# The inverse sums of the decay heads go through DRAM, and the last values step moves into the next head

## The chip, the cores and the metric

The kernel runs on one core of a Trainium2 chip. The metric is the device time of one launch in microseconds, the median of three runs. A core has five engines that run their own instruction streams and meet at semaphores: TensorE (PE; the weight loads are listed as PEld), VectorE (DVE), ScalarE (ACT), GpSimd (POOL) and SyncE (SP), which issues all transfers of this kernel.

## The reference, cut to what matters

The program is a transformer block followed by a two-layer second block over 1024 tokens of width 1024. The change lies in the second layer of the second block, in its attention with forget gates: 16 heads of width 64, causal, with a decay term per key that comes from a running sum of log forget gates.

```python
def forgetting_attention(u, k, v, cum):
    # logit[t,s] = q_t.k_s/sqrt(Dh) + cum[t] - cum[s], causal, swept in 128-query blocks
    ...
        logits = jnp.einsum('bqhd,bkhd->bhqk', qi, k,
                            preferred_element_type=jnp.float32) * scale
        logits = logits + (ci[..., :, None] - cum_k[:, :, None, :])
        ...
        p = jax.nn.softmax(logits, axis=-1)
        return jnp.einsum('bhqk,bkhd->bqhd', p.astype(v.dtype), v)

def mixer_sublayer(x, mem, w_in, w_mem_kv, w_out, main_fn):
    ...
    y_main = main_fn(u_main)
    y_mem = memory_attention(q_mem, mem, w_mem_kv)
    y = jnp.concatenate([y_main * jax.nn.silu(g_main), y_mem * jax.nn.silu(g_mem)], axis=-1)
    return y @ w_out
```

## The kernel before, in words

Everything but the row maxima and row sums is held with features on the partitions. Products are made of float32 numbers split into a high and a low part (`whi`, `wlo` for weights, `Hb[0]`, `Hb[1]` for activations), so that one product is three matmuls (`mm3`, lines 428 to 430). GpSimd splits each weight panel of 128x1024 (`split`, lines 844 and 846) after SP has loaded it (`load_panel`, line 462).

The stage `fox` runs the 16 heads one after the other, about 31.5 us each. A head has 8 query tiles `qt` of 128 queries. For each tile TensorE makes the scores (`scores`, lines 1680 and 1681, with the mask at 1683), VectorE takes the row maximum against the decay row `ncB` (`row_max`, line 3026), ScalarE makes exponentials with their row sums (`exps`, through the helper on line 1815), TensorE turns them back by transposes (`flips`, line 1694), ScalarE copies the high part (`flip_hi`), VectorE makes the low part (`flip_lo`, line 2324), and for each pair of tiles TensorE multiplies by the values (`values(h, p)`, p from 0 to 3, line 1708). The result of a pair lies in two halves of one PSUM bank; ScalarE copies one (`other_half`), VectorE adds both into `Y32` (`add`, line 2327). Two heads share one 128-partition block of `Y32`.

Between these steps TensorE is filled with steps of later projections: `fill(n)` takes n steps of three matmuls each from the tiles that make the next keys, queries and gates. How many stand where is written in the table `FILL` (24 per head, 4 of them behind the first scores), and `FILL_LAST` (16) for the last two heads. Evacuating these tiles is `project` on ScalarE and VectorE; its last step for a key half is the cast on line 2998.

At the end of a head VectorE takes the reciprocals of the 8 row sums of each partition (line 3078, `inv_sum`, which lies in `stat_pool`). Queries are on partitions there but along the free dimension in `Y32`. So TensorE makes 8 transposes of broadcast columns (`inverse_rows`, line 1717) into two banks of PSUM, then `values(h, 3)` follow, and VectorE multiplies the 64x1024 block of the head by the turned rows (line 2327, second use). After two heads `gate(i)` (line 3048) multiplies the 128x1024 block by its gate; it stands behind query tile 1 of the next even head.

SP's queue in a head holds the values of the next head (`Vx`, line 793), a weight panel, and the decay row of the next head (`ncB`, line 798), which may go only when the head's last row maximum is taken. Transfers wait on SP in the order in which they are written.

## Time and profile before

| | us |
|---|---|
| median of 3 runs | 3052.43 (3050.56 to 3052.73) |
| the profiled execution | 3051.6 |
| its span | 3049.8 |

| engine | busy us | share of the span |
|---|---|---|
| PE | 2938.5 | 96% |
| PEld | 2444.0 | 80% |
| DVE | 1519.9 | 50% |
| POOL | 1032.7 | 34% |
| ACT | 923.2 | 30% |

Times on rows are counted from the start of the span. The decay heads run from about 2270 to 2765 us. Matmuls are pipelined: each row of one gives its start and its own length, which overlaps the next one's; what a matmul costs in a row of others is the distance between two starts. "idle before <-releaser" in brackets on a row is a wait and the engine and line that ended it.

### The profile page before, as it was taken

How to read it: one execution, taken by the hardware profiler on the slowest of the kernel's cores; microseconds unless marked ns; L12 is line 12 of the kernel's file. 1: busy time of each engine (PE TensorE's matmuls, PEld its weight loads, DVE VectorE, ACT ScalarE, POOL GpSimd, SP SyncE). 2: the span in 40 equal slices, each digit the busy share in tenths (PEclk: the TensorE clock that was granted, in tenths of full speed). 3: DMA queues.
4: the chain of work that ended last, by engine and by line, in shares of the span. 5: the costliest groups of instructions: out<-in, count | busy, mean ns of one | idle time of the engine just before them, and what ended most of it. 6: DMA issues, size and time to landing. Idle time of an engine off the chain costs nothing.

```text
span 3049.8 us, 37301 instructions
## 1 busy us (share of the span) xinstructions
PE 2938.5 (96%) x14926; PEld 2444.0 (80%) x14926; DVE 1519.9 (50%) x2288; ACT 923.2 (30%) x1606; POOL 1032.7 (34%) x454
## 2 busy tenths in 40 slices
PE   7999999999999999999999999999999999999997
PEld 3877778888887888888888887788788888887786
DVE  5943238887634313132234444545536666664545
ACT  5122226665113101010010111411335555553412
POOL 1333251000586434444444443233331221212241
PEclk9999999999999999999999999999999999999998
DMA  6534584221533111111111111111232212111111
GB/s 243 190 121 140 202 239 117 73 73 42 191 120 111 49 49 48 50 47 51 46 50 47 55 63 49 42 49 42 98 125 63 56 56 63 56 56 43 36 53 63
DMA packets 118090, 256.85 MB, mean 84 GB/s; under 512 B 47228, under 2 KB 69276, under 8 KB 113712
## 3 DMA queue, kind: packets, MB, share of 16 engines
q1 hardware_dynamic: 117936, 254.71, 25.5%
q8 instruction: 107, 1.75, 0.2%
q14 instruction: 47, 0.39, 0.0%
HBM read 210.20 MB, written 45.97 MB: 84 GB/s over the span
## 4 chain that ended last, share of the span: by engine, by line
PE 81%; DVE 8%; ACT 5%; issue 2%; DMA 1%; POOL 1%; SPq 0%; ACTq 0%; DVEq 0%; POOLq 0%
PE ps L428 23%; PE ps L430 23%; PE ps L429 23%; PE ps L1708 2%; ACT tmp L1815 2%; PE ps L1285 2%; PE ps L1694 2%; PE ps L1273 1%; ACT Ea L1815 1%; PE ps L1680 1%; PE ps L1681 1%; DVE tmp L2549 1%; DVE Z L2327 1%; DVE mx L2778 1%; DVE ETb_lo L2324 1%
## 5 line engine op out<-in xcount | busy, mean ns | idle before, releaser
L844 POOL TENSOR_TENSOR whi<-raw,onesf 128x1024 fp32r<-128x1024 f32 x189 | 365.0, 1931 | 1888.7 <-PE ps L430 1766.5
L428 PE MATMUL ps<-Hb_hi,whi 128*128 128x512 f32 x1424 | 573.3, 403 | 10.3 <-DVE Y L2751 5.9
L430 PE MATMUL ps<-Hb_hi,wlo 128*128 128x512 f32 x1424 | 556.4, 391 | 0.0
L429 PE MATMUL ps<-Hb_lo,whi 128*128 128x512 f32 x1424 | 555.5, 390 | 0.0
L846 POOL TENSOR_TENSOR wlo<-raw,whi 128x1024 fp32r<-128x1024 f32 x189 | 504.2, 2668 | 14.8
L428 PEld LDWEIGHTS ps<-Hb_hi,whi 128*128 128x128 f32 x1424 | 268.3, 188 | 62.6 <-issue 8.1
L430 PEld LDWEIGHTS ps<-Hb_hi,wlo 128*128 128x128 f32 x1424 | 267.6, 188 | 57.9
L429 PEld LDWEIGHTS ps<-Hb_lo,whi 128*128 128x128 f32 x1424 | 268.6, 189 | 47.8
L1815 ACT ACTIVATE tmp<-ps 64x256 f32<-64x256 f32 (+2 forms) x97 | 57.8, 596 | 531.9 <-PE ps L430 465.0
L1815 ACT ACTIVATE tmp<-tmp,mx 128x1280 f32<-128x1280 f32 (+2 forms) x192 | 187.2, 975 | 66.9 <-DVE mx L3026 56.8
L428 PE MATMUL ps<-Uhi,whi 128*128 128x512 f32 x512 | 199.2, 389 | 0.0
L429 PE MATMUL ps<-Ulo,whi 128*128 128x512 f32 x512 | 199.2, 389 | 0.0
L430 PE MATMUL ps<-Uhi,wlo 128*128 128x512 f32 x512 | 199.2, 389 | 0.0
L2327 DVE TENSOR_TENSOR tmp<-tmp 128x1024 f32<-128x1024 f32 x44 | 86.1, 1957 | 184.0 <-ACT tmp L1815 183.6
L2698 DVE SCALAR_TENSOR_TENSOR X<-ps,modx,X 128x1024 f32<-128x1024 f32 x32 | 41.1, 1283 | 256.6 <-PE ps L430 256.6
L428 PE MATMUL ps<-Yb_hi,whi 128*128 128x512 f32 (+1 forms) x408 | 153.8, 377 | 0.0
L429 PE MATMUL ps<-Yb_lo,whi 128*128 128x512 f32 (+1 forms) x408 | 153.6, 377 | 0.0
L430 PE MATMUL ps<-Yb_hi,wlo 128*128 128x512 f32 (+1 forms) x408 | 153.6, 377 | 0.0
L428 PE MATMUL ps<-Hhi,whi 128*128 128x512 f32 x384 | 151.9, 395 | 1.0 <-POOL wlo L846 0.8
L429 PE MATMUL ps<-Hlo,whi 128*128 128x512 f32 x384 | 149.6, 390 | 0.0
L430 PE MATMUL ps<-Hhi,wlo 128*128 128x512 f32 x384 | 149.5, 389 | 0.0
L1815 ACT ACTIVATE Ea<-ps 128x512 fp32r<-128x512 f32 (+1 forms) x192 | 87.2, 527 | 83.3 <-PE ps L1273 83.3
(458 smaller groups left out, 5816.9 us busy)
## 6 DMA issues: line engine op xcount, KB each, us to landing
raw<-in_w SPq DMA_DIRECT2D x197, 512.0 KB, 3.5
adas<-in_ada SPq DMA_DIRECT2D x16, 1024.0 KB, 4.9
raw<-in_w SPq DMA_DIRECT2D x44, 256.0 KB, 3.8
adaE<-in_ada SPq DMA_DIRECT2D x4, 2048.0 KB, 23.4
gate_d<-gst SPq DMA_DIRECT2D x16, 512.0 KB, 2.8
v_d<-VS SPq DMA_DIRECT2D x2, 4096.0 KB, 14.9
ncB<-cum_d SPq DMA_DIRECT2D x16, 512.0 KB, 3.5
Vx<-v_d SPq DMA_DIRECT2D x16, 512.0 KB, 4.5
```

The costliest lines, as they stand in the source:

```text
L428: nc.tensor.matmul(o, wh, xh, start=start, stop=False)
L429: nc.tensor.matmul(o, wh, xl, start=False, stop=False)
L430: return nc.tensor.matmul(o, wl, xh, start=False, stop=stop)
L844: nc.gpsimd.tensor_tensor(whi[b][:, 0:w], raw[b][:, 0:w], onesf[:, 0:1].to_broadcast([P, w]), ALU.mult).then_inc(S("split_hi"), 1)
L846: nc.gpsimd.tensor_tensor(wlo[b][:, 0:w], raw[b][:, 0:w], f32(whi[b][:, 0:w]), ALU.subtract).then_inc(S("split"), 1)
L1273: last = nc.tensor.transpose(ps[:, c:c + P], tmp[t % 2][:, P * kt:P * kt + P], ident[:, :])
L1285: last = nc.tensor.matmul(o, Va[h % 2][:, kt, :], Ea[u % 2][n][:, kt, :], start=kt == 0 and n == 0, stop=kt == 9 and n == 1)
L1694: last = nc.tensor.transpose(ps[:, b + P * (kt - 4 * x):b + P * (kt - 4 * x) + P], tmp[qt % 2][:, P * kt:P * kt + P], ident[:, :])
L1708: last = nc.tensor.matmul(ps[:, 5 * HALF + c0:5 * HALF + CTX], Vx[h % 2][:, kt, :], E[x][:, kt, c0:CTX], start=kt == 0 and x == 0, stop=kt ...
L1815: nc.scalar.activation(dst, src, func, **kw).then_inc(sem, 1)
L2327: nc.vector.tensor_tensor(o, a, b, op).then_inc(sem, 1)
L2698: nc.vector.scalar_tensor_tensor(X1[:, k, :], g, modx[:, 40 + k:41 + k], X1[:, k, :], ALU.mult, ALU.add).then_inc(free, 1)
```

## The change

Heads 0 to 14 no longer turn their inverse sums on TensorE. SP stores the 128x8 reciprocals of a head into a row of DRAM (`inv_d`) in the order of the queries, and loads them back broadcast over 64 partitions, 256 queries at a time, into spare columns of `rs` and `acc` (`rowB`), two pieces for each half of the queries. GpSimd multiplies `Y32` by them in four pieces of 64x256 (`normalise`), placed between its weight splits (`heads_beside`). The second half's loads wait until GpSimd has used the first half's.

`values(h, 3)` now stands in head h + 1, behind its first scores and two of the four projection steps there; `other_half(h, 3)` and `add(h, 3)` move with it on ScalarE and VectorE. `gate(i)` moves from query tile 1 to the end of query tile 7 of the same head and waits for GpSimd's multiplies. Head 15 keeps its transposes and its multiply on VectorE.

```diff
+                def store_inverse(h):
+                    sp.wait_ge(S("fx_inv"), h + 1)
+                    sp.dma_start(inv_d[h].rearrange("(t p) -> p t", p=P), inv_sum[:, 8 * (h % 2):8 * (h % 2) + 8], allow_slow_non_contiguous=True).then_inc(S("row_stored"), 16)
+
+                def inverse_rows(h, half):
+                    r = slice(64 * (h % 2), 64 * (h % 2) + 64)
+                    if half == 0:
+                        sp.wait_ge(S("row_stored"), 32 + 16 * (h + 1))
+                    if h or half:
+                        sp.wait_ge(S("fx_norm"), 4 * h + 2 * half)
+                    for x in range(2):
+                        c = HALF * half + CTX * x
+                        sp.dma_start(rowB[x][r, :], inv_d[h:h + 1, c:c + CTX].to_broadcast([64, CTX])).then_inc(S("inv_row"), 16)
...
                 for h in range(FOX):
+                    if h:
+                        store_inverse(h - 1)
                     if h + 1 < FOX:
                         head_values(h + 1)
+                    if h:
+                        inverse_rows(h - 1, 0)
                     if h % 2 == 0:
+                        if h:
+                            inverse_rows(h - 1, 1)
                         load_panel("fox", 25, 0, kq_panel(h + 1))
                     elif h + 1 < FOX:
                         load_panel("fox", 25, 0, gate_panel(h // 2 + 1))
+                        inverse_rows(h - 1, 1)
+                    else:
+                        inverse_rows(h - 1, 1)
                     if h + 1 < FOX:
                         head_decay(h + 1)
...
+            def normalise(h, half, last_split):
+                r = slice(64 * (h % 2), 64 * (h % 2) + 64)
+                gp.wait_ge(S("inv_row"), 32 * (2 * h + half + 1))
+                gp.wait_ge(S("fx_out"), 3 * (4 * h + 2 * half + 2))
+                gp.wait_ge(S("split"), last_split + 1)
+                for x in range(2):
+                    c = slice(HALF * half + CTX * x, HALF * half + CTX * x + CTX)
+                    y = Y32[r, h // 2, c]
+                    nc.gpsimd.tensor_tensor(y, y, rowB[x][r, :], ALU.mult).then_inc(S("fx_norm"), 1)
+                    gp.wait_ge(S("fx_norm"), 4 * h + 2 * half + x + 1)
+
+            def heads_beside(p0):
+                for m in range(2, 4):
+                    split(p0 + m)
+                for i in range(8):
+                    if i:
+                        normalise(2 * i - 1, 0, p0 + 3 * i + 3)
+                        normalise(2 * i - 1, 1, p0 + 3 * i + 3)
+                    split(p0 + 3 * i + 4)
+                    if i < 7:
+                        split(p0 + 3 * i + 5)
+                    normalise(2 * i, 0, p0 + (3 * i + 5 if i < 7 else 25))
+                    normalise(2 * i, 1, p0 + (3 * i + 5 if i < 7 else 25))
+                    split(p0 + (3 * i + 6 if i < 7 else 26))
...
-                        if h and c == 1:
-                            pe.wait_ge(S("fx_inv"), 3 * h)
...
-                        if qt < 7:
+                        if qt == 0 and h:
+                            fill(2)
+                            values(h - 1, 3)
+                            fill(share[0] - 2)
+                        elif qt < 7:
                             fill(share[qt])
...
-                    inverse_rows(h)
-                    if h == FOX - 1:
-                        next(ahead)
-                    values(h, 3)
+                inverse_rows(FOX - 1)
+                next(ahead)
+                values(FOX - 1, 3)
...
                 def gate(i):
-                    dve.wait_ge(S("fx_inv"), 3 * (2 * i + 2))
+                    dve.wait_ge(S("fx_norm"), 4 * min(2 * i + 2, FOX - 1))
...
                         if qt == 0:
                             for x in before:
                                 project(*x)
+                            if h:
+                                add(h - 1, 3)
...
-                        if qt == 1 and h % 2 == 0 and h:
+                        if qt == 7 and h % 2 == 0 and h:
                             gate(h // 2 - 1)
                     x = slice(8 * (h % 2), 8 * (h % 2) + 8)
                     dve.wait_ge(S("fx_e"), 8 * h + 8)
+                    if h >= 2:
+                        dve.wait_ge(S("row_stored"), 32 + 16 * (h - 1))
                     nc.vector.reciprocal(inv_sum[:, x], row_sum[:, x]).then_inc(S("fx_inv"), 1)
                     for x in range(2):
                         flip_lo(h, 7, x)
-                    add(h, 3)
-                    dve.wait_ge(S("fx_inv"), 3 * h + 2)
-                    dve.wait_ge(S("fx_out"), 3 * (4 * h + 4))
-                    tt(Y32[r, h // 2, :], Y32[r, h // 2, :], ps[r, HALF:HALF + T], ALU.mult, S("fx_inv"))
```

TensorE's order at the end of head 1 and the start of head 2, before (L1694 flips, L1717 the transposes of the inverse sums, L1708 values, L1680 to L1683 scores, L428 to L430 one projection step):

```order
L1694 MATMUL ps<-ident,tmp 128x128 x8
L428 MATMUL ps<-Hb_hi,whi 128x512
L429 MATMUL ps<-Hb_lo,whi 128x512
L430 MATMUL ps<-Hb_hi,wlo 128x512
L1717 MATMUL ps<-ident,stat_pool 128x128 x8
L1708 MATMUL ps<-ETb_hi,Vx_189 128x256
L1708 MATMUL ps<-ETb_lo,Vx_189 128x256
...
L1680 MATMUL ps<-K_0_184,Q_0_182 128x128
L1681 MATMUL ps<-K_0_186,Q_0_182 128x128
L1683 MATMUL ps<-mrow_60,identr 128x128
L428 MATMUL ps<-Hb_hi,whi 128x512
```

The same place after (L1744 flips, L1758 values, L1730 to L1733 scores, L430 to L432 one projection step):

```order
L1744 MATMUL ps<-ident,tmp 128x128 x8
L430 MATMUL ps<-Hb_hi,whi 128x512
L431 MATMUL ps<-Hb_lo,whi 128x512
L432 MATMUL ps<-Hb_hi,wlo 128x512
L1730 MATMUL ps<-K_0_184,Q_0_182 128x128
L1731 MATMUL ps<-K_0_186,Q_0_182 128x128
L1733 MATMUL ps<-mrow_60,identr 128x128
L430 MATMUL ps<-Hb_hi,whi 128x512
...
L1758 MATMUL ps<-ETb_hi,Vx_189 128x256
L1758 MATMUL ps<-ETb_lo,Vx_189 128x256
```

The transposes are gone, and between the last projection step of head 1 and the sixteen value matmuls stand the first scores of head 2 and two projection steps.

VectorE's order at the end of head 2 and the start of head 3, before (L2998 the cast, L3078 the reciprocal, L2324 the low parts, L2327 the addition and then the multiply, L3026 the row maximum of head 3):

```order
L2998 CAST K_1_187<-K_1_187 64x512
L3078 RECIPROCAL stat_pool<-mxf 128x8
L2324 TENSOR_TENSOR ETb_lo<-ps,ETb_hi 128x4x128 x2
L2327 TENSOR_TENSOR Y_167<-ps,tmp 64x256
L2327 TENSOR_TENSOR Y_167<-Y_167,ps 64x1024
L3026 ISA tmp,mx<-ps,ncB 128x128
L3026 ISA mx 128x1
L3012 SCALAR_TENSOR_TENSOR acc<-acc,ps 128x512
```

The same place after (L3053 the cast, L3105 the gate, L3138 the reciprocal, L2379 the low parts, L3081 the row maximum, L2382 the addition):

```order
L3053 CAST K_1_187<-K_1_187 64x512
L3105 SCALAR_TENSOR_TENSOR Y_167<-Y_167,acc 128x1024
L3138 RECIPROCAL stat_pool<-mxf 128x8
L2379 TENSOR_TENSOR ETb_lo<-ps,ETb_hi 128x4x128 x2
L3081 ISA tmp,mx<-ps,ncB 128x128
L3081 ISA mx 128x1
L3067 SCALAR_TENSOR_TENSOR acc<-acc,ps 128x512
L2382 TENSOR_TENSOR Y_167<-ps,tmp 64x256
```

The gate has come in ahead of the reciprocal, the multiply is gone, and the addition stands behind head 3's first row maximum and a projection's evacuation.

SP's order in head 2, after (L804 the store of head 1's reciprocals, L795 the values of head 3, L814 the broadcast loads, L464 a weight panel, L800 the decay row of head 3):

```order
L804 DMA inv_d<-stat_pool 128x8x1
L795 DMA Vx_189<-v_d 128x1024
L814 DMA rs<-inv_d 64x256
L814 DMA acc<-inv_d 64x256
L814 DMA rs<-inv_d 64x256
L814 DMA acc<-inv_d 64x256
L464 DMA raw<-in_w 128x1024
L800 DMA ncB<-cum_d 128x1024
```

Before, the values, the panel and the decay row stood there alone.

## Rows read from the trace of the kernel before

**Rows 1.** The page, part 1: busy us of each engine (share) xinstructions.

```profile
PE 2938.5 (96%) x14926; PEld 2444.0 (80%) x14926; DVE 1519.9 (50%) x2288; ACT 923.2 (30%) x1606; POOL 1032.7 (34%) x454
```

**Rows 2.** Stretch: length, busy PE, PEld, DVE, ACT, POOL (instructions), clock, DMA.

```profile
2334.00:2366.00 32.00, 31.93 (x193) 27.88 (x192) 20.63 (x51) 17.75 (x39) 4.85 (x3) 1.00 0.17 56
```

**Rows 3.** Line 1717: count, duration ns min/median/max, first and last start us.

```profile
L1717 PE MATMUL ps<-ident,stat_pool x128: 271/273/323, 2292.8 to 2765.7; 128*128 128x128 f32 x128
```

**Rows 4.** Timeline of TensorE, seam of heads 1 and 2: start us, us, instruction.

```profile
2324.22 1.04 PE L1717 MATMUL ps<-ident,stat_pool 128*128 128x128 f32 x8
2325.33 0.38 PE L1708 MATMUL ps<-ETb_hi,Vx 128*128 128x256 f32 x1
...
2327.28 0.27 PE L1680 MATMUL ps<-K,Q 128*128 128x128 f32 x1
...
2327.61 0.45 PE L428 MATMUL ps<-Hb_hi,whi 128*128 128x512 f32 x1
...
2329.05 0.39 PE L428 MATMUL ps<-Hb_hi,whi 128*128 128x512 f32 x1
```

**Rows 5.** The chain that ended last, same seam: start us, us, what.

```profile
2323.35 0.61 ACT ETb_hi L1815
2323.98 1.30 DVE ETb_lo L2324 x2
```

**Rows 6.** Timeline of SP and VectorE, seam of heads 1 and 2.

```profile
2321.10 0.33 SPq L798 DMA_DIRECT2D ncB<-cum_d  x1
...
2323.24 0.42 DVE L2998 CAST K<-K 64x512 fp32r<-64x512 f32 x1
...
2329.22 1.26 SPq L462 DMA_DIRECT2D raw<-in_w  x2
```

**Rows 7.** Timeline of GpSimd, VectorE and TensorE, seam of heads 2 and 3.

```profile
2342.67 1.90 POOL L844 TENSOR_TENSOR whi<-raw,onesf 128x1024 fp32r<-128x1024 f32 x1 [13.47 <-PE ps L430]
...
2354.80 0.42 DVE L2998 CAST K<-K 64x512 fp32r<-64x512 f32 x1
...
2355.25 0.20 DVE L3078 RECIPROCAL stat_pool<-mxf 128x8 f32<-128x8 f32 x1
...
2355.55 1.29 DVE L2324 TENSOR_TENSOR ETb_lo<-ps,ETb_hi 128x512 fp32r<-128x512 f32 x2
...
2355.79 1.04 PE L1717 MATMUL ps<-ident,stat_pool 128*128 128x128 f32 x8
2356.89 0.38 PE L1708 MATMUL ps<-ETb_hi,Vx 128*128 128x256 f32 x1
```

**Rows 8.** Timeline of VectorE: the gate multiply of the first pair.

```profile
2333.46 1.22 DVE L3048 SCALAR_TENSOR_TENSOR Y<-Y,rs 128x1024 f32<-128x1024 f32 x1
```

**Rows 9.** Timeline of VectorE and TensorE, seam of heads 14 and 15.

```profile
2733.04 0.42 DVE L2998 CAST K<-K 64x512 fp32r<-64x512 f32 x1
...
2733.75 1.09 PE L1717 MATMUL ps<-ident,stat_pool 128*128 128x128 f32 x8 [0.45 <-DVE stat_pool L3078]
...
2736.88 0.27 PE L1680 MATMUL ps<-K,Q 128*128 128x128 f32 x1
```

**Rows 10.** GpSimd's groups by shape: count, busy us, mean ns, idle before.

```profile
L844 POOL TENSOR_TENSOR whi<-raw,onesf 128x1024 fp32r<-128x1024 f32 x189 | 365.0, 1931 | 1888.7 <-PE ps L430 1766.5 <-DMA raw<-in_w 96.0 <-DVE Hb_lo L2324 26.2
...
L862 POOL TENSOR_TENSOR rsr<-raw,onesf 128x1024 fp32r<-128x1024 f32 x1 | 2.9, 2877 | 0.0
L864 POOL TENSOR_TENSOR tmpr<-raw,rsr 128x512 fp32r<-128x512 f32 x2 | 2.6, 1294 | 0.2
L864 POOL TENSOR_TENSOR QN_lo<-raw,rsr 128x1024 fp32r<-128x1024 f32 x1 | 2.4, 2392 | 0.1
```

**Rows 11.** DMA issues: count, KB each, median us from issue to landing.

```profile
raw<-in_w SPq DMA_DIRECT2D x44, 256.0 KB, 3.8
...
ncB<-cum_d SPq DMA_DIRECT2D x16, 512.0 KB, 3.5
...
v_d<-vst SPq DMA_DIRECT2D x5, 1024.0 KB, 6.7
```

More of the change, by code:

```diff
@@ L340, in build @@
         SG = (rs, acc)
+        rowB = (rs[:, T:KEYS], acc[:, T:KEYS])
         neg_max, row_sum, inv_sum = mx, mxf, stat_pool
@@ L364, in build @@
         cum_d = scratch("cum_d", FOX, T)
+        inv_d = scratch("inv_d", FOX, T)
         wb_d, w64_d, wf_d = scratch("wb_d", P, 8, 2 * P), scratch("w64_d", 96, T), scratch("wf_d", 8, P, 4, P)
@@ L642, in sp_program @@
                         sp.wait_ge(S("rates"), 9)
-                        sp.dma_start(rate_d.rearrange("h (t p) -> (h t) p", p=P), krows[0:NH * 10, :]).then_inc(S("rate_stored"), 16)
+                        sp.dma_start(rate_d.rearrange("h (t p) -> (h t) p", p=P), krows[0:NH * 10, :]).then_inc(S("row_stored"), 16)
             if on("mla"):
@@ L666, in sp_program @@
                 sp.wait_ge(S("kr_stored"), 32)
-                sp.wait_ge(S("rate_stored"), 16)
+                sp.wait_ge(S("row_stored"), 16)
                 sp.wait_ge(S("wf_moved"), STAGED)
@@ L780, in sp_program @@
                 load_panel("foxw", 4, 0, 0)
-                sp.wait_ge(S("cum"), 1)
-                sp.dma_start(cum_d, ncum[0:FOX, :]).then_inc(S("cum_stored"), 16)
+                sp.wait_ge(S("gate_log"), 4)
+                sp.dma_start(cum_d, ncum[0:FOX, :]).then_inc(S("row_stored"), 16)
                 for j in range(1, 4):
@@ L786, in sp_program @@
                 sp.dma_start(v2_d[1], f32(VS[1][:, :, :, :])).then_inc(S("fx_vst"), 16)
-                sp.wait_ge(S("cum_stored"), 16)
+                sp.wait_ge(S("row_stored"), 32)
             if on("fox"):
@@ L922, in pool_program @@
                         splits(stage, 0, 12 - SPLIT_LEAD)
+                    elif stage == "fox":
+                        heads_beside(P0["fox"])
                     elif stage == "out1":
@@ L1439, in mem_tiles @@
                             elif l:
-                                pe.wait_ge(S("fx_inv"), 3 * FOX)
+                                pe.wait_ge(S("fx_inv"), FOX + 2)
                             c = slice(HALF * x, HALF * x + HALF)
@@ L1712, in inverse_rows @@
                 def inverse_rows(h):
-                    pe.wait_ge(S("fx_inv"), 3 * h + 1)
+                    pe.wait_ge(S("fx_inv"), h + 1)
                     pe.wait_ge(S("fx_x"), CHUNKS * h + CHUNKS)
@@ L2268, in project @@
                     else:
-                        act.wait_ge(S("cum"), 1)
+                        act.wait_ge(S("gate_log"), 4)
                         if x >= 2:
@@ L2310, in act_program @@
                                 project(*x)
+                            if h:
+                                other_half(h - 1, 3)
                         if qt in (2, 5) and mine:
@@ L2313, in act_program @@
                     flip_hi(h, 7)
-                    other_half(h, 3)
+                other_half(FOX - 1, 3)
             if on("mem2"):
@@ L2981, in dve_program @@
                 dve.wait_ge(S("gate_log"), 3)
-                nc.vector.tensor_tensor_scan(ncum[r, :], rs[r, 0:T], acc[r, 0:T], 0.0, ALU.mult, ALU.add).then_inc(S("cum"), 1)
+                nc.vector.tensor_tensor_scan(ncum[r, :], rs[r, 0:T], acc[r, 0:T], 0.0, ALU.mult, ALU.add).then_inc(S("gate_log"), 1)
                 token_values(1)
@@ L3045, in gate @@
                 def gate(i):
-                    dve.wait_ge(S("fx_inv"), 3 * (2 * i + 2))
+                    dve.wait_ge(S("fx_norm"), 4 * min(2 * i + 2, FOX - 1))
+                    if i == 7:
+                        dve.wait_ge(S("fx_inv"), FOX + 2)
                     dve.wait_ge(S("fx_g"), 2 * i + 2)
@@ L3052, in dve_program @@
                 for h in range(FOX):
-                    r = slice(64 * (h % 2), 64 * (h % 2) + 64)
                     before = projections(h - 1)[2:] if h else []
@@ L3065, in dve_program @@
                                 project(*x)
+                            if h:
+                                add(h - 1, 3)
                         if qt == 2 and mine:
@@ L3080, in dve_program @@
                         flip_lo(h, 7, x)
-                    add(h, 3)
-                    dve.wait_ge(S("fx_inv"), 3 * h + 2)
-                    dve.wait_ge(S("fx_out"), 3 * (4 * h + 4))
-                    tt(Y32[r, h // 2, :], Y32[r, h // 2, :], ps[r, HALF:HALF + T], ALU.mult, S("fx_inv"))
+                add(FOX - 1, 3)
+                dve.wait_ge(S("fx_inv"), FOX + 1)
+                dve.wait_ge(S("fx_out"), 12 * FOX)
+                tt(Y32[64:128, 7, :], Y32[64:128, 7, :], ps[64:128, HALF:HALF + T], ALU.mult, S("fx_inv"))
                 gate(7)
```

## The prediction

> **What bounds the kernel now.** I read the page's busy shares first: TensorE is busy 96% of the 3049.8 us, VectorE 50%, ScalarE 30%, GpSimd 34% [rows 1]. The change touches only the stage with the sixteen decay heads, so the next view is that of a stretch: between 2334 and 2366 us (one head and a bit) TensorE is busy 31.93 of 32.00 us at full granted clock, while VectorE works 20.6 us, ScalarE 17.8 us and GpSimd 4.9 us [rows 2]. A microsecond taken from TensorE's row is worth a microsecond here, as long as nothing else becomes late; a microsecond taken from VectorE or given to GpSimd is worth nothing by itself.
>
> Third, the seam between two heads, in order of time. Each head ends with eight transposes of the inverse sums (L1717, sixteen times eight of them, 273 ns each [rows 3]). Matmuls are pipelined, so their price is not 8 x 273 ns = 2.18 us but the distance between starts: the transposes at 2324.22, the first value matmul at 2325.33 [rows 4]. That is 1.11 us from the transposes' start to the values' start. And the transposes are not even what the values wait for: the chain that ended last goes through ScalarE's copy of the last flips (2323.35) and VectorE's two subtractions (2323.98, 1.30 us), and then to the values [rows 5]. The reader is to see in this that deleting the transposes alone would gain nothing at such a seam, since the values would still start at about 2325.3. It is the second part of the change, values moved behind the next head's first scores, that makes the 1.11 us free.
>
> **What is removed and moved on TensorE.** Fifteen of sixteen heads lose the eight transposes; the last head keeps them. At fifteen seams the values step now stands behind the next head's first scores and two projection steps. These three are no new work: the scores took 2327.61 - 2327.28 = 0.33 us, the two steps 2329.05 - 2327.61 = 1.44 us [rows 4]. So TensorE, at 2324.22, does the scores and two steps and comes to the values at 2324.22 + 0.33 + 1.44 = 2325.99, when the subtractions, over at 2323.98 + 1.30 = 2325.28, have long released them [rows 5]. It asks for them 0.7 us after they are free. The whole 1.11 us is gained (1.10 at the seam between heads 2 and 3 [rows 7]), provided that the next head's scores may start 3.06 us earlier than before. They need the last cast of the keys: 2323.24 + 0.42 = 2323.66, 0.56 us before TensorE wants it [rows 6]. The first row maximum then needs the decay row, whose transfer is issued at 2321.10 [rows 6] and lands 3.5 us later [rows 11], at 2324.6, before VectorE is free (2325.3). The exponentials it feeds are wanted by the next flips only some 4 us on. So no new wait at a seam of this kind.
>
> **The gate multiply, moved.** On VectorE the gate (128x1024, 1.22 us [rows 8]) leaves the second query tile of heads 2, 4 ... 14 for the end of the eighth, ahead of the reciprocal and of the last subtractions. There it is in the way. At the seam behind head 2 the cast ends at 2355.22; with the gate behind it (2356.44), the reciprocal (0.20, 2356.64) and the subtractions (1.29) end at 2357.93 instead of 2356.84 [rows 7]. TensorE comes to the values at 2355.79 + 0.33 + 1.44 = 2357.56. It waits about 0.4 us, so that 1.10 - 0.4 = 0.7 us is left. That holds for heads 2 to 12, six seams.
>
> Head 14 has fewer projection steps, and TensorE waits there already: the transposes stood back 0.45 us for the reciprocal, the values step ended at 2736.88 [rows 9], and scores and two steps would have been done at 2736.88 + 0.33 + 1.44 = 2738.65. Now: cast until 2733.46, gate until 2734.68, reciprocal 2734.88, subtractions 2736.15, values (1.95 us, from 2325.33 to 2327.28 in [rows 4]) until 2738.15. The gain is 0.5 us.
>
> **The multiply by the inverse sums** leaves VectorE (64x1024 per head) and needs no cover: VectorE is busy two thirds of the time here [rows 2]. On GpSimd it becomes four multiplies of 64x256 per head, a shape that the trace does not have. A two-input op takes 1294 ns for 512 elements and 2392 ns for 1024 [rows 10], that is 2.14 ns per element and, carried down, 0.75 us for 256; bounds are 0.6 us (half of 1294) and 1.3 us. Four are 3.0 us a head. GpSimd waited 13.5 us for TensorE before the split at 2342.67 [rows 7], so the splits keep room. No TensorE time.
>
> **The way through DRAM.** SP now issues per head one store of 128x8 values, four bytes each, and four loads of 64 rows. Behind the waiting SP stand the next weight panel and the next head's decay row. The even heads are the tight ones: the store of head h-1 stands behind the panel loads, issued at 2329.22 for 1.26 us [rows 6], so it starts at 2330.5. Nearest row for 1024 short pieces: a quarter-megabyte panel in 256-byte pieces lands in 3.8 us; a store of one megabyte takes 6.7 us [rows 11]. I take 3.8 and keep 3 and 6.7. Then 2334.3; the first two rows land by 2337.8 (at most the decay row's 3.5 us), two multiplies until 2339.3, the other two rows 2342.8, two multiplies 2344.3. The gate asks for them at 2355.2 [rows 7]. There are 10.9 us to spare, so nothing is lost for any store under 3.8 + 10.9 = 14.7 us. The odd heads' chain ends ahead of the decay row's issue, which is a whole head later. Cost on the path: nothing.
>
> **The sum.** Eight seams without a gate (behind heads 0, 1, 3, 5 ... 13) x 1.10 = 8.8; six x 0.7 = 4.2; one x 0.5. Together 13.5 us. The profiled execution took 3051.6 us (span 3049.8), hence 3038.1; the median of the three runs is 0.8 above it, so the median should be 3038.5 to 3039. I say **3038.5**, 0.45% faster.
>
> **A rule that speaks against it.** The trace has a split of 128x1024 on GpSimd that took 2877 ns where the same op takes about 1930 in the mean [rows 10], so GpSimd does get held up by about 0.95 us elsewhere in the program. The Trainium skill, SBUF — State Buffer, section SBUF: two separate sides, says that GpSimd and VectorE share a port pair as an exclusive lock, taken for a whole instruction, which VectorE wants in a 2-port mode or with two SBUF inputs; its gate multiply is such an instruction. By that rule the gate would be blocked if a multiply of GpSimd ran at that moment. No row of the decay heads shows a collision.
>
> **Rivals.** (a) *The seam fills up again.* The values leave the wait, but the cover is thin: 0.56 us between cast and scores, 0.7 us between subtractions and values. If the subtractions come 1.0 us later against TensorE than I count (ScalarE does the next exponentials sooner, VectorE the next maxima), each seam loses 0.3 us without a gate and 1.0 with one: 8 x 0.3 + 7 x 1.0 = 9.4, leaving 4 us, time 3048; half of that gives 3043. For it: TensorE follows VectorE closely at each seam [rows 5]. Against it: VectorE sheds 1.22 + 1.2 us in each pair's early part. (b) *The DRAM chain comes too late,* the slower side. If four-byte stores cost over 14.7 us, VectorE stands at the gate with the last subtractions and the next maximum behind it, and TensorE behind those, in seven heads. At 20 us: 7 x 5.3 = 37 us lost, 13.5 gained, 3076. At 16.6 us it breaks even. For it: no row has four-byte pieces. Against: 1024 pieces of 256 bytes need 3.8 us. (c) *Collisions on VectorE:* if a multiply of GpSimd holds the gate for 0.75 us in seven heads, 7 x 0.75 = 5.3 us go, time 3044. Against: by the chain above GpSimd is done ten microseconds earlier. (d) *The gate costs nothing,* if the subtractions wait for ScalarE in any case: 15 x 1.1 = 16.5, time 3035.5.
>
> **How the numbers follow.** Forecast 0.62; (a) 0.15, of which a third ends within 0.2%; (b) 0.08; (c) 0.05; (d) 0.10. The range takes in the forecast, (d), (c) and the milder half of (a): 3034.5 to 3046. What a measurement can tell from no change is 0.2%, 6.1 us, so faster means below 3046.3. Faster 0.85, same 0.07, slower 0.08.
>
> **What would show it.** L1717's successor with 8 transposes instead of 128. From the last projection matmul of a head to the next head's first scores 0.2 us. A wait of TensorE for VectorE's subtractions of about 0.4 us in even heads and none in odd ones. The store landing in 3 to 7 us, and GpSimd's multiplies at 0.75 us, over by the middle of the head. VectorE idle at the gate for DMA or GpSimd would prove (b); cast and gate longer than 0.42 and 1.22 us would prove (c); waits for the subtractions at every seam, (a). The forecast is wrong at its root if a head still takes 31.5 us, the distance from 2324.22 to 2355.79 [rows 4, 7].

## The result, and the profile after

| | us |
|---|---|
| before, median of 5 runs | 3050.66 (3047.43 to 3052.73) |
| after, median of 5 runs | 3063.78 (3062.64 to 3067.46) |
| ratio | 1.0046 (95%: 1.0035 to 1.0058) |
| the profiled execution of after; its span | 3066.08; 3064.3 |

The change costs 13 us; the prediction's sum was a gain of 13.5 us. The page of after, part 1 and the line on packets in part 2, beside [rows 1]:

```profile
PE 2930.4 (96%) x14806; PEld 2437.3 (80%) x14806; DVE 1519.1 (50%) x2273; ACT 922.6 (30%) x1606; POOL 1078.3 (35%) x514
...
DMA packets 138490, 260.84 MB, mean 85 GB/s; under 512 B 63788, under 2 KB 89676, under 8 KB 134112
```

TensorE has 120 instructions and 8 us of work less, in a span 14.5 us longer. So it idles more, and the question is where. The best ruler is the distance between the ends of two heads, each end taken as the start of the last row of eight flips on TensorE's timeline (L1694 before, L1744 after): head 3 stands for the distance from head 2's end to head 3's. Fifteen distances in each trace, in us:

| | head 1 | head 2 | head 3 | head 5 | head 7 | heads 9, 11 | sum of 15 |
|---|---|---|---|---|---|---|---|
| before | 31.45 | 31.56 | 31.46 | 31.45 | 31.45 | 31.4 | 471.5 |
| after | 30.27 | 30.58 | 40.70 | 38.79 | 40.66 | 31.3 | 487.2 |

Odd seams (behind heads 1, 3 ...) gained 1.0 to 1.6 us each (2.6 behind head 13), about what was promised or more. The loss sits at the even seams, between an even head and the next odd one, above all at the first three. The waits of after between 2270 and 2790 us (engine, line, releaser: us in total, times, longest):

```profile
POOL Y L885 <- DMA acc<-inv_d: 180.0, 27, 15.6
...
DVE tmp L3081 <- DMA ncB<-cum_d: 34.3, 7, 8.7
...
PE ps L1744 <- ACT tmp L1868: 19.6, 7, 5.7
...
PE ps L1758 <- DVE ETb_lo L2379: 10.2, 7, 2.2
```

VectorE stands seven times, 34 us in all, before the first row maximum of an odd head, because the decay row is not there. Behind the first three of these waits TensorE stands for the exponentials, 15.9 us in all (and 0.4 us behind head 14; the other three waits of that line, 3.3 us at heads 14 and 15, stand in the kernel before too). In all seven places it waits for the subtractions. GpSimd's own 180 us are the cause of nothing by their size; it is their place that matters. The chain that ended last in after, from the odd seam to the even one (start us, us, what):

```profile
2323.11 1.91 POOL whi L869
2325.08 2.42 POOL wlo L871
2327.51 0.58 SPq L464
2328.14 0.67 SPq L464
2328.85 9.80 DMA inv_d<-stat_pool
2338.67 0.48 SPq L814
2339.20 3.12 DMA acc<-inv_d
2342.38 0.75 POOL Y L885
2343.21 0.75 POOL Y L885
2343.97 0.45 SPq L814
2344.46 3.29 DMA acc<-inv_d
2347.87 0.73 POOL Y L885
2348.69 0.74 POOL Y L885
2349.50 1.91 POOL whi L869
2351.47 2.39 POOL wlo L871
2353.88 0.34 SPq L464
2354.27 11.11 DMA ncB<-cum_d
2365.40 0.29 DVE tmp L3081
```

This is the working of the prediction's DRAM part, row for row, with two differences. The store takes 9.80 us and not 3.8. And the chain does not end at the gate: GpSimd's split of the next panel (L869, L871) stands in GpSimd's order behind the four multiplies, SP's next panel load (L464) waits for that split to free the raw buffer, and the decay row stands in SP's queue behind the panel. So the decay row is issued at 2354.27, 2.5 us after the head's last flips began (2351.78); at the odd seam before it went at 2319.62, 1.6 us ahead of them (2321.20). And it then takes 11.11 us to land instead of 3.5 [rows 11].

VectorE and TensorE at that seam (timeline of after; idle time and releaser in brackets):

```profile
2351.47 2.38 POOL L871 TENSOR_TENSOR wlo<-raw,whi 128x1024 fp32r<-128x1024 f32 x1
2351.93 0.42 DVE L2382 TENSOR_TENSOR Y<-ps,tmp 64x256 f32<-64x256 f32 x1 [0.65 <-ACT tmp L1868]
2352.38 1.76 DVE L3053 CAST K<-K 64x512 fp32r<-64x512 f32 x1
...
2356.72 0.39 PE L1758 MATMUL ps<-ETb_hi,Vx 128*128 128x256 f32 x1 [1.50 <-DVE ETb_lo L2379]
...
2365.40 0.29 DVE L3081 CUSTOM_DVE_ANT_0 tmp<-ps,ncB 128x128 f32<-128x128 f32 x1 [8.74 <-DMA ncB<-cum_d]
...
2366.29 0.47 PE L1744 MATMUL ps<-ident,tmp 128*128 128x128 f32 x1 [5.72 <-ACT tmp L1868]
```

The cast took 0.42 us before [rows 7] and 1.76 now: it ends at 2354.14, 0.28 us after GpSimd's split (2353.86). Then TensorE's clock (stretches of after; columns as in rows 2):

```profile
2358.00:2366.00 8.00, 2.57 (x17) 2.16 (x15) 0.30 (x2) 0.26 (x1) 0.00 (x0) 0.97 0.58 46
2366.00:2370.00 4.00, 3.71 (x10) 2.94 (x11) 1.56 (x5) 1.98 (x7) 0.00 (x0) 0.50 0.34 86
2370.00:2374.00 4.00, 4.00 (x17) 3.35 (x16) 0.99 (x3) 1.10 (x4) 1.90 (x1) 0.71 0.00 0
2374.00:2378.00 4.00, 4.00 (x21) 3.38 (x20) 1.94 (x4) 1.75 (x4) 3.75 (x3) 1.00 0.02 4
```

After the 5.72 us of idleness the granted clock is 0.50 (1.2 GHz) and it is back at 1.00 (2.4 GHz) after 2372: two projection matmuls stood 0.43 us apart until then, 0.23 after it. Six microseconds at half speed cost 3.

The 40.70 us of head 3 are so accounted for: a wait for the subtractions of 1.50 us where the kernel without the way through DRAM (the first experiment below) has 0.16, so 1.3 more, as much as the cast is longer (1.76 - 0.42); 5.7 of idleness; 3.0 of half clock; together 10.0. An undisturbed head of this kind takes 30.7 there, and 40.7 - 30.7 = 10.0.

### The profile page after: what moved, and what is told of

Its sections match the earlier page's. It is cut to its first block, busy times and chain, and to the rows that moved or that the text cites. A ratio compares the mean times of both kernels' runs of the same rounds, so it can differ in the third digit from the quotient of the medians.

```text
span 3064.3 us, 37209 instructions
## 1 busy us (share of the span) xinstructions
PE 2930.4 (96%) x14806; PEld 2437.3 (80%) x14806; DVE 1519.1 (50%) x2273; ACT 922.6 (30%) x1606; POOL 1078.3 (35%) x514
## 2 busy tenths in 40 slices
DMA packets 138490, 260.84 MB, mean 85 GB/s; under 512 B 63788, under 2 KB 89676, under 8 KB 134112
## 4 chain that ended last, share of the span: by engine, by line
PE 75%; DVE 9%; DMA 5%; ACT 5%; issue 3%; POOL 2%; SPq 1%; ACTq 0%; DVEq 0%; POOLq 0%
PE ps L430 22%; PE ps L432 21%; PE ps L431 21%; ACT tmp L1868 2%; PE ps L1337 2%; PE ps L1744 1%; PE ps L1325 1%; PE ps L1758 1%; DMA inv_d<-stat_pool 1%; DMA ncB<-cum_d 1%; ACT Ea L1868 1%; DVE tmp L2604 1%; DMA acc<-inv_d 1%; POOL wlo L871 1%; PE ps L1730 1%
## 5 line engine op out<-in xcount | busy, mean ns | idle before, releaser
L869 POOL TENSOR_TENSOR whi<-raw,onesf 128x1024 fp32r<-128x1024 f32 x189 | 366.2, 1937 | 1676.7 <-PE ps L432 1552.5
L430 PE MATMUL ps<-Hb_hi,whi 128*128 128x512 f32 x1424 | 576.5, 405 | 10.3 <-DVE Y L2806 5.9
L432 PE MATMUL ps<-Hb_hi,wlo 128*128 128x512 f32 x1424 | 558.6, 392 | 0.0
L871 POOL TENSOR_TENSOR wlo<-raw,whi 128x1024 fp32r<-128x1024 f32 x189 | 504.0, 2667 | 14.8
L430 PEld LDWEIGHTS ps<-Hb_hi,whi 128*128 128x128 f32 x1424 | 270.0, 190 | 62.4 <-issue 8.1
L432 PEld LDWEIGHTS ps<-Hb_hi,wlo 128*128 128x128 f32 x1424 | 268.8, 189 | 58.5
L430 PE MATMUL ps<-Uhi,whi 128*128 128x512 f32 x512 | 199.2, 389 | 0.0
L432 PE MATMUL ps<-Uhi,wlo 128*128 128x512 f32 x512 | 199.2, 389 | 0.0
L2382 DVE TENSOR_TENSOR tmp<-tmp 128x1024 f32<-128x1024 f32 x44 | 86.1, 1957 | 184.1 <-ACT tmp L1868 183.6
L430 PE MATMUL ps<-Yb_hi,whi 128*128 128x512 f32 (+1 forms) x408 | 153.8, 377 | 0.0
L432 PE MATMUL ps<-Yb_hi,wlo 128*128 128x512 f32 (+1 forms) x408 | 153.6, 377 | 0.0
L430 PE MATMUL ps<-Hhi,whi 128*128 128x512 f32 x384 | 152.1, 396 | 0.5 <-POOL wlo L871 0.2
L432 PE MATMUL ps<-Hhi,wlo 128*128 128x512 f32 x384 | 149.5, 389 | 0.0
L3081 DVE CUSTOM_DVE_ANT_0 tmp<-ps,ncB 128x512 f32<-128x512 f32 (+3 forms) x128 | 75.0, 586 | 98.0 <-PE ps L1733 51.8
```

Source lines behind the costliest of these rows:

```text
L430: nc.tensor.matmul(o, wh, xh, start=start, stop=False)
L432: return nc.tensor.matmul(o, wl, xh, start=False, stop=stop)
L869: nc.gpsimd.tensor_tensor(whi[b][:, 0:w], raw[b][:, 0:w], onesf[:, 0:1].to_broadcast([P, w]), ALU.mult).then_inc(S("split_hi"), 1)
L871: nc.gpsimd.tensor_tensor(wlo[b][:, 0:w], raw[b][:, 0:w], f32(whi[b][:, 0:w]), ALU.subtract).then_inc(S("split"), 1)
L2382: nc.vector.tensor_tensor(o, a, b, op).then_inc(sem, 1)
L3081: nc.vector.tensor_tensor_reduce(tmp[qt % 2][:, c0:c1], ps[:, b:b + c1 - c0], ncB[:, c0:c1], -1.0, col_ if x else 3e38, ALU.add, ALU.min, ...
```

## The experiments

Three theories. **A, the order:** the decay row is late since it stands behind a panel load that waits for a split that waits for the multiplies. **B, the store:** 1024 pieces of four bytes take too long, and slow the transfers beside them. **C, the collision:** the split that comes late now runs beside VectorE's last cast (and gate), which then stand until it ends. All ratios are against the kernel before on the same chip. Times on rows of different kernels have no common zero inside the decay heads (head 1's last flips begin at 2322.66 before and at 2321.20 in after), so where two kernels are compared, places are given from the start of a head's last flips.

**The seam alone.** The changed kernel without store, loads and GpSimd's multiplies:

```diff
-                        store_inverse(h - 1)
...
-                        inverse_rows(h - 1, 0)
...
-                            inverse_rows(h - 1, 1)
...
-                        normalise(2 * i - 1, 0, p0 + 3 * i + 3)
...
-                    dve.wait_ge(S("fx_norm"), 4 * min(2 * i + 2, FOX - 1))
+                    dve.wait_ge(S("fx_out"), 3 * (4 * (2 * i + 1) + 4))
```

> The changed kernel without the way of the inverse sums: no store, no broadcast loads, no multiply on GpSimd (so heads 0 to 14 are left undivided), the gate waits for nothing but the additions. The order on TensorE and VectorE is that of the change. If the prediction's step on the seams holds and all the loss is in the chain through DRAM, this gains the 13.5 us that I forecast, ratio to before 0.9956, TensorE waits about 0.4 us for the subtractions in even heads, and the cast takes 0.42 us. If the new seam itself costs time (maxima and exponentials late), it stays above 0.998 with waits at most seams.

3035.23 us, 0.9947 (0.9930 to 0.9963), 16.7 us faster. Heads take 30.25 to 30.27 us where no gate stands at the seam (30.57 once, behind head 1) and 30.64 to 30.69 where one does (the last two, with fewer projection steps, apart), 454.1 in sum against 471.5. Heads 0 to 14 stay undivided here. The half of the change that lies on TensorE is worth all that was forecast and more; all that went wrong is in the way through DRAM.

**The transposes alone.** The kernel before with one transpose in place of eight in heads 0 to 14; VectorE multiplies these heads by 1.0 instead of the turned rows, so they stay undivided:

```diff
-                    for qt in range(8):
+                    for qt in (range(8) if h == FOX - 1 else range(1)):
```

> The kernel before, with one transpose of the inverse sums instead of eight in heads 0 to 14 and nothing moved. VectorE multiplies these heads by 1.0 instead of the turned rows (so they stay undivided), a shorter operation that nothing waits for. It tests the step that deleting the transposes alone gains nothing: the values step still waits for the subtractions, heads' ends stay 31.5 us apart, time 3050. If the transposes were on the path by themselves, seven of them less at 0.11 us each give 15 x 0.8 = 12 us, time 3038.

3051.27 us against 3051.52, 0.9998 (0.9988 to 1.0007), heads 472.0 in sum. The reading of [rows 5] holds: TensorE merely waits where it transposed (L1708 for L2324, 12.5 us in 15 waits).

**Order on SP (A without C).** In even heads the decay row goes ahead of the panel:

```diff
-                        load_panel("fox", 25, 0, kq_panel(h + 1))
...
                         head_decay(h + 1)
-                        if h % 2:
-                            load_panel("fox", 25, 0, kq_panel(h + 1))
+                        load_panel("fox", 25, 0, kq_panel(h + 1))
```

> The changed kernel, with one move on SP: in even heads the next decay row is issued ahead of the weight panel. Theory A (SP's queue: the decay row stands behind a panel load that waits for GpSimd's late split): the row is issued at the head's last maximum, 4 us sooner, lands in about 3.5 us, VectorE waits for it nowhere; the 16 us of TensorE waiting for exponentials and some 8 us at the low clock go, time about 3041. Theory B (the transfer itself is stretched to 10 us or more by the four-byte store issued behind it): the landing stays near 10 us, VectorE still waits 3 to 5 us in three heads, time above 3052. Under both the cast stays stretched to 1.8 us and TensorE waits 1.5 us for the subtractions in even heads.

3058.58 us, 1.0027 (1.0017 to 1.0036). The decay row is issued at 2351.48 and nobody waits for it any more, yet only 5 of the 28 us between the change and the seam alone came back (8 of the 33 us by the distances: 478.9 in sum). Its timeline at two even seams:

```profile
2353.15 2.38 POOL L869 TENSOR_TENSOR wlo<-raw,whi 128x1024 fp32r<-128x1024 f32 x1
...
2353.61 2.20 DVE L3051 CAST K<-K 64x512 fp32r<-64x512 f32 x1
...
2355.85 1.22 DVE L3103 SCALAR_TENSOR_TENSOR Y<-Y,rs 128x1024 f32<-128x1024 f32 x1
...
2358.40 0.39 PE L1756 MATMUL ps<-ETb_hi,Vx 128*128 128x256 f32 x1 [1.94 <-DVE ETb_lo L2377]
...
2613.23 0.52 DVE L3051 CAST K<-K 64x512 fp32r<-64x512 f32 x1
...
2613.54 2.46 POOL L869 TENSOR_TENSOR wlo<-raw,whi 128x1024 fp32r<-128x1024 f32 x1
2613.78 3.31 DVE L3103 SCALAR_TENSOR_TENSOR Y<-Y,rs 128x1024 f32<-128x1024 f32 x1
...
2618.41 0.38 PE L1756 MATMUL ps<-ETb_hi,Vx 128*128 128x256 f32 x1 [2.30 <-DVE ETb_lo L2377]
```

Either the cast stands (2.20 us instead of 0.42, over 0.28 us after the split's end at 2355.53), or, where the split begins a little later, the cast goes in between the two ops of the split and the gate stands (3.31 instead of 1.22, over 1.09 after 2616.00). The first happens behind heads 2 and 12, the second behind the other five. Each time the subtractions behind them are late by about the same amount, and TensorE waits 17.5 us in seven places. Six of these waits are followed by 3.4 us at half clock, with less idleness than in after (1.9 to 3.2 us each). The stretch behind the first of them, columns as in rows 2:

```profile
2358.00:2366.00 8.00, 7.60 (x36) 6.69 (x37) 2.33 (x8) 2.24 (x7) 0.00 (x0) 0.79 0.49 53
```

A head costs 34.0 to 35.1 us in five of the seven places (32.2 and 33.2 in the others) where 30.7 would do. So A's own wait is a part of the loss, but taking it away lets C's grow, from 10.2 to 17.5 us of waits for the subtractions, and some 23 of the 28 us stay.

By the Trainium skill (SBUF — State Buffer, section SBUF: two separate sides) GpSimd and VectorE hold a shared port pair for whole instructions, which VectorE needs in its 2-port modes and with two SBUF inputs. The trace agrees: cast and gate stand, while the addition at 2351.93 above, whose one input is in PSUM, took its usual 0.42 us beside the split.

**A store of 128 pieces (B).** The reciprocals are stored in the order in which they lie, 32 bytes per partition; this kernel's inverse rows are in the wrong order of queries.

```diff
-                    sp.dma_start(inv_d[h].rearrange("(t p) -> p t", p=P), inv_sum[...
+                    sp.dma_start(inv_d[h].rearrange("(p t) -> p t", p=P), inv_sum[...
```

> The changed kernel with the store laid out by partition: 128 pieces of 32 bytes instead of 1024 of 4 bytes. The rows that come back are in another order, so the output is not the reference's. If the four-byte pieces are what costs 9.8 us, the store lands in 2 to 3 us, the chain ends 7 us sooner, the split starts by 2344 and the decay row goes at the last maximum; no wait for it, no cast beside a split, time 3037 to 3040. If instead the write to DRAM and the wait for it cost most of the 9.8 us whatever the pieces, the landing stays above 7 us and the time near 3060.

3036.20 us, 0.9952 (0.9935 to 0.9969). DMA issues of it and of after, 2260 to 2790 us (count, KB each, median us to landing):

```profile
Vx<-v_d SPq DMA_DIRECT2D x15, 512.0 KB, 3.8
...
inv_d<-stat_pool SPq DMA_DIRECT2D x15, 4.0 KB, 1.9
```

```profile
inv_d<-stat_pool SPq DMA_DIRECT2D x15, 4.0 KB, 9.8
Vx<-v_d SPq DMA_DIRECT2D x15, 512.0 KB, 9.7
```

The same 4 KB land in 1.9 us instead of 9.8, the values beside them in 3.8 instead of 9.7, and the whole loss is gone: the multiplies end at 2341.55 and the split begins at 2341.62. That is 20.7 us behind the start of head 1's last flips, where after has 28.3, the kernel before 20.0 and the kernel with the seam alone, without any multiplies, 18.7.

**The store away from the decay row (B).** The store goes behind the values of the next head, so that it does not run beside the decay row:

```diff
-                    if h:
-                        store_inverse(h - 1)
                     if h + 1 < FOX:
                         head_values(h + 1)
+                    if h:
+                        store_inverse(h - 1)
```

> The changed kernel with the store of the inverse sums behind the load of the next values on SP, instead of ahead of it; the panel and the decay row keep their places. Behind an even head the store then goes about 3 us later, when the decay row has had 4.6 us. Theory B (the store beside it stretches the decay row): the row lands in about 5 us instead of 10 to 11, VectorE's waits of 7.5 to 8.7 us fall to about 3. Theory A (only the late issue counts): landing stays at 10 to 11 us, no change. The chain starts 1 us later in odd heads, so the issue of the decay row is no earlier. Time: 3055 under B, 3064 under A.

3068.98 us, 1.0052 (1.0036 to 1.0069): a miss for the time. The decay row behind head 2, issued at 2356.31, was used at 2360.96, 4.65 us later; the landings of the seven rows are 4.2 to 6.1 us, where the first three of after have 9.9 to 11.1. So the store beside it does stretch its landing. But the store itself now takes 11.1 us in the median beside the values, the panel behind the split leaves 4.5 us behind the start of head 2's last flips instead of 2.1 in after, and what was gained in the wait for the decay row (26.5 us in seven, from 34.3) went into the wait for the subtractions (18.9 us, from 10.2).

**Order on GpSimd (A at its root).** The four-byte store stays; the split goes between the two halves of the multiply, alone and together with the decay row first:

```diff
                         normalise(2 * i - 1, 0, p0 + 3 * i + 3)
-                        normalise(2 * i - 1, 1, p0 + 3 * i + 3)
                     split(p0 + 3 * i + 4)
+                    if i:
+                        normalise(2 * i - 1, 1, p0 + 3 * i + 4)
```

> The changed kernel with the one move on GpSimd alone: the split of the even heads between the two halves of the multiply. SP's order is the change's. If the root is the split that stands behind the whole multiply, this alone brings the panel load, the decay row (issued at the last maximum, near 2350) and the cast back into place: the decay row then has the panel 3 us ahead of it and the four-byte store 5 us behind it and lands in under 5 us; time 3036 to 3039. If SP's order is a cause of its own, waits of VectorE for the decay row of 2 us or more stay and the time is above 3043.

> The changed kernel with two moves: the decay row ahead of the panel load on SP in even heads, and on GpSimd the even heads' split between the two halves of the multiply instead of behind both. The four-byte store stays and lands in about 10 us. Theory C (what is left of the loss once the decay row is on time is the split that now runs beside VectorE's cast and the clock that falls after TensorE's wait): the split is over by 2350, the cast takes 0.42 us before the seam, TensorE waits under 0.5 us for the subtractions, clock as before, time 3036 like the kernel without the chain. Theory D (the slow store itself holds TensorE or VectorE up): still 3050 or more.

Alone 3035.30 us, 0.9951 (0.9935 to 0.9968); with both 3034.27, 0.9943 (0.9927 to 0.9960). GpSimd, SP and VectorE of the first at the even seam (timeline):

```profile
2344.98 2.38 POOL L871 TENSOR_TENSOR wlo<-raw,whi 128x1024 fp32r<-128x1024 f32 x1
...
2347.39 0.34 SPq L464 DMA_DIRECT2D raw<-in_w  x1
...
2347.78 0.43 SPq L800 DMA_DIRECT2D ncB<-cum_d  x1
...
2349.56 0.42 DVE L3054 CAST K<-K 64x512 fp32r<-64x512 f32 x1
```

Two lines moved, and the store may be as slow as it likes (10.8 us here): the split is over 2.2 us before the cast, which takes 0.42 us again, and the decay row leaves SP 1.8 us ahead of the cast, where after has it 1.9 us behind. VectorE still waits for the decay row twice in the first kernel (3.3 us together), TensorE never because of it. The intervals of the two overlap; the second move adds nothing that can be told.

**The slow store in the kernel before.** Only the store and its waits are added:

```diff
+                    if h:
+                        sp.wait_ge(S("fx_inv"), 3 * (h - 1) + 1)
+                        sp.dma_start(inv_d[h - 1].rearrange("(t p) -> p t", p=P), ...
```

> The kernel before, with nothing but the store of the inverse sums added, 1024 pieces of four bytes per head, at the place of SP's queue where the change has it; nobody reads it. It prices the store by itself. Expected: it lands in 9 to 11 us, with nothing of the chain around it; the values' load issued behind it takes 9 to 10 us instead of 4.5, which nobody waits for; decay rows, issued ahead of it, land in 3.5 us; time as before, 3051. If the store holds up the decay row also when nothing else is late, the row's landing goes above 6 us and VectorE waits for it.

3051.60 us, 0.9997 (0.9987 to 1.0006). The store lands in 10.9 us and makes the values land in 10.5 instead of 4.4, and nobody waits. A slow transfer by itself costs nothing here; what hangs on it does.

**A good short store.** As with the 128 pieces above, but GpSimd reads its operands with the matching stride, so that all of the computation is there (each piece then covers part of every query tile, so the multiplies wait for all four additions of the head); and the same with the gate behind the last subtractions:

```diff
+                    p_ = 64 * half + 32 * x
+                    y = Y32[r, h // 2, :].rearrange("f (t p) -> f t p", p=P)[:, :, p_:p_ + 32]
+                    row = rowB[x][r, :].rearrange("f (p t) -> f t p", t=8)
...
-                        if qt == 7 and h % 2 == 0 and h:
-                            gate(h // 2 - 1)
...
                         flip_lo(h, 7, x)
+                    if h % 2 == 0 and h:
+                        gate(h // 2 - 1)
```

> The changed kernel with a store of 128 pieces of 32 bytes, and GpSimd picking the queries back into order in its multiply: 64 rows of 8 x 32 elements, the inverse sums read with a stride of 8. Each piece covers 32 queries of every tile, so the first half waits for all four additions. The output is the reference's. Expected: store 1.9 us as in the run with the long store, multiply 0.75 us, or up to 1.5 if GpSimd is slower with strides, which nothing waits for; time 3036, ratio 0.995. If the strided multiply takes over 3 us each, the split moves late again and the time is above 3045.

> The kernel of the run before, with the gate of the even heads behind the last subtractions instead of ahead of the reciprocal. It prices the gate at its place: the distance of heads' ends was 30.67 us for even heads against 30.26 for odd ones without the chain. If the gate is the 0.4 us, the two become equal and seven seams give 2.8 us, time 3033.5. If the next head's first maximum, now 1.2 us later, is waited for, the even heads stay at 30.67 or grow.

3034.10 us, 0.9945 (0.9928 to 0.9961), the multiplies 0.90 to 0.91 us instead of 0.73; and **3030.22 us**, 0.9933 (0.9916 to 0.9949), the lowest median of all, 20 us under the kernel before; its interval overlaps with those of the next two kernels. With the gate last the even seams fall from 30.65 to 30.27 us, so the gate ahead of the subtractions cost 0.4 us each.

**Late split and slow store, but room behind them (C).** Decay row first and gate last, the split as late as in after; and the same with the last cast on ScalarE (only this move is shown; the other two are as above):

```diff
+                        if qt == 7 and mine and mine[1][0] == "kq":
...
+                            act.wait_ge(S("fx_kqd"), 4 * kx + 2 * ks + 1)
+                            copy(K2[kx % 2][64:128, kc], f32(K2[kx % 2][0:64, kc]), S("fx_kd2"))
...
-                    else:
+                    elif part == 2:
```

> The same without the move of the cast: decay row first, gate behind the subtractions, cast on VectorE. It separates the two. The cast still ends only when GpSimd's operation ends, so I expect it at 1 to 2.2 us in even heads; the subtractions follow 1.1 us sooner than with the gate ahead of them, TensorE waits 0.5 to 2 us, time 3038 to 3045. If the cast is held up by something else than GpSimd (the gate behind it, a queue), it falls to 0.42 us.

> The run with the decay row first (3058.6), where the split of the even heads still runs late, at the end of the eighth tile, with both VectorE operations that got stuck beside it taken away from the place ahead of the subtractions: the last cast of a head is done by ScalarE, and the gate stands behind the subtractions. The split and the four-byte store stay as they were. If what holds the seam is VectorE's copy held up by GpSimd's split, TensorE's waits for the subtractions (1.6 to 3.2 us, seven times) and the low clock behind them go, time 3032 to 3036. If the late split or the slow store hurts in another way, 3045 or more stays.

3033.04 us, 0.9936 (0.9919 to 0.9952), and 3032.05, 0.9934 (0.9917 to 0.9950). The second confirms C: no VectorE instruction that the split can hold stands before the subtractions, and all even seams of heads 2 to 12 take 30.3 us. The store is as slow as before: its trace has no landing times of it, but the first broadcast load, which waits for it, goes 10.1 to 13.6 us behind its issue. The first came out better than I had expected (3038 to 3045). Its timeline:

```profile
2352.89 1.89 POOL L867 TENSOR_TENSOR whi<-raw,onesf 128x1024 fp32r<-128x1024 f32 x1
...
2354.49 0.57 DVE L3051 CAST K<-K 64x512 fp32r<-64x512 f32 x1
...
2354.86 2.47 POOL L869 TENSOR_TENSOR wlo<-raw,whi 128x1024 fp32r<-128x1024 f32 x1
...
2355.22 1.29 DVE L2377 TENSOR_TENSOR ETb_lo<-ps,ETb_hi 128x512 fp32r<-128x512 f32 x2
2356.43 1.98 DVE L3103 SCALAR_TENSOR_TENSOR Y<-Y,rs 128x1024 f32<-128x1024 f32 x1
```

The last multiplies ended 0.8 us later against the cast than in the kernel with only the decay row first (2352.81 and 2354.49 here, 2351.11 and 2353.61 there), so the cast slips in between the two ops of the split, as it did at five seams there, and is held for 0.15 us only. At six of seven seams it took 0.42 to 0.74 us; at the seventh, behind head 14, it took 2.23, and TensorE waited 1.7 us. The long hold fell on the gate (1.98 us), which no longer stands before anything that TensorE needs soon. So this kernel shows what the gate's place is worth, and also that its good time hangs on a phase of under a microsecond.

## Why the prediction was wrong, point by point

*The bound and the seam* were right. TensorE is the bound; deleting the transposes alone gains nothing; moving the values behind the next scores frees the seam. The sum was 13.5 us and the heads with the seam alone gained 17.4. Seams without a gate mostly gave 1.2 to 1.3 us (1.0 behind head 1), not 1.1, and one with a gate 0.8, not 0.7 (31.45 to 30.66). The last two distances, to the ends of heads 14 and 15, where there are fewer projection steps, gave 2.7 and 1.0 (31.20 to 28.54, 30.47 to 29.45), for which the sum had 1.1 and 0.5. In the first of the two TensorE also idles 0.9 us less than before (1.5 against 2.4 us); the rest is open.

*The gate ahead of the subtractions:* 0.4 us a seam forecast, 0.4 measured (30.64 to 30.69 with it, 30.27 without). Right.

*GpSimd's multiply:* 0.75 us forecast, 0.73 measured. Right. "So the splits keep room" was wrong: it looked at GpSimd's idle time, 13.5 us, and not at the split as somebody's deadline.

**The step that failed is "Cost on the path: nothing" in the way through DRAM.** It has two faults, and the second one is the graver:

- The store was put at 3.8 us, 6.7 at most, by rows of 256-byte pieces and of a megabyte; it takes 9.8. By the prediction's own working this alone was covered: anything under 14.7 us was to be free.
- The 14.7 came from a single consumer, the gate at 2355.2. The change also put the split behind the multiplies, and behind the split, on SP, the panel and the decay row. The last multiply ended at 2349.43, 3.4 us before the gate was due (the cast, unheld, would have been over at 2352.80), as a store of 9.8 us was allowed to; but the split, which had begun 20.0 us behind the start of head 1's last flips (2342.67 [rows 7]), began 28.3 us behind it (2349.50). The prediction names panel and decay row as what stands behind the waiting SP, and then prices neither. "No new wait" for the decay row was worked out at the odd seam, from its issue at 2321.10 [rows 6], and never asked of the even one.

*Rival (b), the chain too late,* was the right kind of case with the wrong deadline: it was to break even at 16.6 us of store, and a store of 9.8 us cost 33 us at the even seams. *Rival (c), collisions,* had the right mechanism and the chance of 0.05. It was turned down because "GpSimd is done ten microseconds earlier", which held for the multiplies in the forecast and not for the split behind them. What stands is first the cast, and the gate where the split begins later.

*What was to show it:* "VectorE idle at the gate for DMA or GpSimd would prove (b)". There is no such idle time; the gate took 1.23 us, and the loss was one place further on. The sign for (c), "cast and gate longer than 0.42 and 1.22 us", did appear: the cast took 1.0 to 2.2 us at the seven even seams. Two more signs failed: the store did not land in 3 to 7 us, and the multiplies ended 2.4 us before the last flips of the head and not by its middle.

The loss adds up: 487.2 against 454.1 with the seam alone, 33.1 us at the seven even seams, of which 28 in the first three. Why the decay row lands after 9.9 to 11.1 us behind heads 2, 4 and 6 and after 4.4 to 5.1 behind the later ones (behind head 8: issued 2564.54, used 2568.97), with the same neighbours in the queue, is open; moving the store away (4.65 us behind head 2) shows that the store beside it has a part in it.

## What to carry to other kernels

When work is put into an engine's queue with a wait in front, list every instruction behind it until the next idle time, and for each who needs its result by when, through the other queues too; the deadline is the earliest of these, not that of the new work's own reader. Where an order is written by hand, put the step that others wait for between the halves of the new one: two lines here, 28 us. On a path with a slow transfer, leave instructions that GpSimd can hold (casts, products of two SBUF operands) behind those that TensorE waits for.

## What the runs showed of the hardware

A store from SBUF of 4 KB in 1024 pieces of four bytes landed in 8.8 to 13.7 us, in 128 pieces of 32 bytes in 1.4 to 3.5 us (medians 1.9, 2.1 and 2.7 in three kernels). The page counts 13,440 packets less in the latter, 15 x 896. Transfers of 512 KB issued beside the former landed in up to 13.8 us (the values 9.7 in the median of after, 4.4 in before).

```profile
DMA packets 125050, 260.84 MB, mean 86 GB/s; under 512 B 50348, under 2 KB 76236, under 8 KB 120672
```

That line is from the page of the kernel with the ordered 32-byte store; after has 63788 under 512 B. The Trainium skill (DMA: Bandwidth & Descriptors, section Specifications) wants 512 bytes a piece for full rate; both stores are far under it, and yet differ by five times.

A VectorE instruction that an op of GpSimd held ended 0.28 us (cast, 0.42 alone) or 1.08 to 1.09 us (gate, 1.22 alone) after that op's end at every place in all these traces where it was late, however early it was due: at most 0.14 us of its work stood beside the op. The casts at the start of even heads, too, take 1.26 us in after instead of 0.42, and TensorE has no wait there.
